# Pool stage: the expert sums of the last two token tiles by two VectorE operations each, one of them ahead of the first pooling

## The reference

```python
y = lax.map(run_block, (xin, blk_e)).reshape(P, D)               # experts, each token's two rows
out = jnp.zeros((N, D), x.dtype).at[tok_pad].add(y * w_pad[:, None])   # sum of the two, by their gates
...
h = layer_norm(DEEPNORM_ALPHA * h + ffn, ln_g[i, 1], ln_b[i, 1])
...
u = (x @ w_in).reshape(B, S, N_POOL_GROUPS, POOL_GROUP_DIM)      # pool_mixer, x is that h
for g, w in enumerate(POOL_WINDOWS):                             # windows of 2, 4, 8, 16 tokens
    ...
    mean = (cs - lag) / jnp.minimum(count, float(w))[None, :, None]
    feats.append(mean - ug)
y = jnp.einsum('bsgc,gcd->bsgd', p, w_grp).reshape(B, S, D_MODEL) * ls
```

## Time and profile before

| | |
|---|---|
| median of 3 runs | 3607.46 us (3605.31 to 3608.38) |
| profiled execution, its own time | 3608.5 us |
| its span in the profile | 3606.6 us |
| PE, DVE, ACT busy, share of the span | 95%, 67%, 52% |
| stage with the change | about 1293 to 1509 us of the span |

### The profile page before, as it was taken

One profiled execution on the slowest core, in us unless ns is written; L12 is line 12 of the kernel. 1 busy time (PEld: TensorE's weight loads), 2 busy tenths in 40 slices (PEclk: granted clock), 3 DMA queues, 4 the chain that ended last, 5 costly groups with the idle time before them and its releaser, 6 DMA issues. The chain is left out here.

```text
span 3606.6 us, 53860 instructions
## 1 busy us (share of the span) xinstructions
PE 3428.8 (95%) x18205; PEld 2678.3 (74%) x18205; DVE 2410.1 (67%) x3983; ACT 1873.4 (52%) x3187; POOL 430.8 (12%) x499
## 2 busy tenths in 40 slices
PE   8998889899999989998999999899999999999988
PEld 7885658688888845686888887477887768787866
DVE  3226877699998957647999888664077655416776
ACT  3215662288888821114888887232167633215764
POOL 0000002011111130000111111410000310000032
PEclk9999999899999999998999999999999999999999
DMA  6643225299999976544999998643242333424142
GB/s 242 227 149 95 71 79 187 93 384 388 378 373 377 360 268 245 199 176 164 381 384 378 378 371 328 235 150 137 72 124 75 128 131 131 168 72 127 43 159 70
DMA packets 416290, 766.17 MB, mean 212 GB/s; under 512 B 107609, under 2 KB 166641, under 8 KB 414072
## 3 DMA queue, kind: packets, MB, share of 16 engines
q1 hardware_dynamic: 393080, 711.93, 55.3%
q0 software_dynamic: 22752, 50.93, 3.8%
q10 hardware_dynamic: 288, 1.05, 0.1%
HBM read 643.00 MB, written 152.72 MB: 221 GB/s over the span
## 5 line engine op out<-in xcount | busy, mean ns | idle before, releaser
L253 DVE TENSOR_TENSOR experts_gate_lo<-weights_gate,experts_gate_hi 128x1024 fp32r<-128x1024 f32 x256 | 301.5, 1221 | 71.5 <-ACT experts_gate_hi L249 71.1
L253 DVE TENSOR_TENSOR experts_down_lo<-weights_down,experts_down_hi 128x1024 fp32r<-128x1024 f32 x256 | 296.2, 1219 | 34.2 <-ACT experts_down_hi L249 34.2
L249 ACT CAST experts_gate_hi<-weights_gate 128x1024 fp32r<-128x1024 f32 x256 | 255.7, 1056 | 110.3 <-DMA weights_gate<-in_moe_w_gate_dram 75.2
L253 DVE TENSOR_TENSOR experts_up_lo<-weights_up,experts_up_hi 128x1024 fp32r<-128x1024 f32 x256 | 295.9, 1218 | 0.3
L318 PE MATMUL project_acc<-project_wh,project_hh 128*128 128x512 f32 (+2 forms) x768 | 286.7, 373 | 0.0
L320 PE MATMUL project_acc<-project_wh,project_hl 128*128 128x512 f32 (+2 forms) x768 | 282.9, 368 | 0.0
L319 PE MATMUL project_acc<-project_wl,project_hh 128*128 128x512 f32 (+2 forms) x768 | 282.9, 368 | 0.0
L249 ACT CAST experts_up_hi<-weights_up 128x1024 fp32r<-128x1024 f32 x256 | 256.0, 1057 | 11.1 <-DMA weights_up<-in_moe_w_up_dram 9.3
L249 ACT CAST experts_down_hi<-weights_down 128x1024 fp32r<-128x1024 f32 x256 | 253.8, 1053 | 6.9 <-DMA weights_down<-in_moe_w_down_dram 6.8
L2855 ACT COPY project_row<-project_acc 128x512 f32<-128x512 f32 (+2 forms) x96 | 51.8, 540 | 365.8 <-PE project_acc L320 365.8
L318 PE MATMUL experts_gp<-experts_gate_hi,experts_xh 128*128 128x512 f32 x512 | 202.4, 395 | 10.9 <-DVE experts_xl L253 10.9
(11 more groups left out here) (560 smaller groups left out, 8190.9 us busy)
## 6 DMA issues: line engine op xcount, KB each, us to landing
weights_gate<-in_moe_w_gate_dram SPq DMA_DIRECT2D x256, 512.0 KB, 11.9
weights_up<-in_moe_w_up_dram SPq DMA_DIRECT2D x256, 512.0 KB, 13.2
weights_down<-in_moe_w_down_dram SPq DMA_DIRECT2D x256, 512.0 KB, 11.4
scratch_y<-qkv_zero SPq DMA_DIRECT2D x48, 512.0 KB, 4.4
pool_shared<-in_ada_w_dram SPq DMA_DIRECT2D x16, 1536.0 KB, 7.9
scratch_proj<-project_row SPq DMA_DIRECT2D x64, 256.0 KB, 2.0
head_store<-in_attn_w_qkv_dram SPq DMA_DIRECT2D x48, 256.0 KB, 3.5
scratch_qkv<-qkv_row SPq DMA_DIRECT2D x48, 256.0 KB, 2.0
```

Of the source, the lines that this page charges most:

```text
L249: return act.copy(hi, src)
L253: return dve.tensor_tensor(lo, src, hi.bitcast(F32), ALU.subtract)
```

## The change

For tiles 6 and 7 the diagonal matrices and the PE sums are gone. ACT scales the loaded h by ALPHA in place (`scale_h`), ahead of copy_u 0 and copy_u 1 in its list. DVE then forms r from SBUF by two operations of 1024 columns, the second on the result of the first. DVE's list is in another order: norm 5 directly behind norm 4, then tile 6's add, window 0, norm 6, tile 7's add, window 1, norm 7, outputs 0, window 2. The modulation's first load waits for the adds and no longer for the PE sums, which stands in the list behind the last store as before.

```diff
+    def scale_h(self, act, i):
+        u = i % self.HB
+        act.wait_ge(self.h_in[u], 16 * (i // self.HB) + 16)
+        act.activation(self.hin[:, u, :], self.hin[:, u, :], ACT.Copy, scale=ALPHA).then_inc(self.h_scaled, 1)
...
-        for c in range(2):
+        if i >= self.DIRECT:
+            v = i % self.YB
+            dve.wait_ge(self.h_scaled, i - self.DIRECT + 1)
+            dve.wait_ge(self.y_in[v], 32 * (i // self.YB) + 32)
+            ch(dve.scalar_tensor_tensor(r, self.yin[v][:, 0, :], self.gates[:, 0, i:i + 1], self.hin[:, u, :], ALU.mult, ALU.add))
+            ch.wait()
+            dve.scalar_tensor_tensor(r, self.yin[v][:, 1, :], self.gates[:, 1, i:i + 1], r, ALU.mult, ALU.add).then_inc(self.r_taken, 2)
+        for c in range(2 if i < self.DIRECT else 0):
...
-                            sp.wait_ge(cb.rp_ready, 2 * TILES)
+                            sp.wait_ge(cb.r_taken, 2 * TILES)
...
                     channels(n)
-                    cb.sums(nc, pe, n + 2 + HT)
                     transposes(n + HT)
...
-                for i in range(TILES):
+                for i in range(cb.DIRECT):
                     cb.diagonals(act, i)
...
                 for n in range(STEPS):
+                    if n < TILES - cb.DIRECT:
+                        cb.scale_h(act, n + cb.DIRECT)
                     copy_u(n)
...
+                norm(HT + 1)
+                cb.add(dve, cch, HT + 2)
                 dve.wait_ge(small_in, 16 * (2 * NG + 1))
-                for n in range(2):
-                    window(n)
-                    cb.add(dve, cch, n + HT + 2)
-                    norm(n + HT + 1)
+                window(0)
+                norm(HT + 2)
+                cb.add(dve, cch, HT + 3)
+                window(1)
+                norm(HT + 3)
...
-                        if n == CG:
-                            norm(TILES - 1)
```

More of the change, by code:

```diff
@@ L2022, with __init__ @@
     YB = 3
-    def __init__(self, ph, K, ahead, y, gates, dest_i, out, yin, r, hn, banks, diagonals, narrow=TILES):
-        self.NARROW = narrow
+    def __init__(self, ph, K, ahead, y, gates, dest_i, out, yin, r, hn, banks, diagonals, narrow=TILES, direct=TILES):
+        self.NARROW, self.DIRECT = narrow, direct
         self.K, self.y, self.gates, self.dest_i, self.out = K, y, gates, dest_i, out
@@ L2032, in __init__ @@
         self.rstd, self.half = ph.sb("cb_rstd", [P, 2, 1]), ph.sb("cb_half", [P, 1])
-        (self.idx_ready, self.diag_ready, self.rp_ready, self.r_taken, self.ms_ready, self.rstd_ready,
+        (self.h_scaled, self.idx_ready, self.diag_ready, self.rp_ready, self.r_taken, self.ms_ready, self.rstd_ready,
          self.h_ready, self.own) = (ph.sem(f"cb_{n}") for n in (
-            "idx_ready", "diag_ready", "rp_ready", "r_taken", "ms_ready", "rstd_ready", "h_ready", "own"))
+            "h_scaled", "idx_ready", "diag_ready", "rp_ready", "r_taken", "ms_ready", "rstd_ready", "h_ready", "own"))
         self.y_in = [ph.sem(f"cb_y_in{u}") for u in range(self.YB)]
@@ L2271, in phase_combine_pool @@
         cb = Combine(ph, K, ahead, y, gates, dest_i, out, [yin[:, n] for n in range(Combine.YB)],
-                     [r[:, n] for n in range(2)], [hn[:, n] for n in range(2)], [rp[:, n, :] for n in range(4)], ph.sb("diag", [P, TILES * 2 * P])[:, :], HT)
+                     [r[:, n] for n in range(2)], [hn[:, n] for n in range(2)], [rp[:, n, :] for n in range(4)], ph.sb("diag", [P, TILES * 2 * P])[:, :], HT, TILES - 2)
         yp = rp[:, 0:2, :]
```

## The result

The changed kernel takes 3612.32 us in the median of 22 runs, before 3608.39 in 22 runs: a ratio of 1.0013, 95% interval 1.0007 to 1.0019, so 2.5 to 6.9 us slower. The profiled execution after took 3614.8 us with a span of 3612.6, against 3608.5 and 3606.6.

What follows compares the result with a forecast made beforehand. PE, busy 170.84 of 170.90 us in the stage, was taken as the bound. Outputs 0 3.8 us late plus 2.7 us of low clock gave + 6.5: 3615.0 against the profiled execution, 3614.0 against the median; 8-in-10 range 3609.8 to 3617.

Steps and rivals of the forecast that it cites:

- PE no longer does 6.9 us: On PE, the sums of tiles 6 and 7, 3.44 us each, go; PE reaches outputs 0 6.6 us earlier.
- DVE's chain: DVE's operations up to window 1 end at 1370.4, so outputs 0 start 3.8 us late after PE idles 10.4 us.
- item 2: Before tile 6's add: h lands at 1349.7, 8.7 us after issue, ACT scales in 1.07 us, DVE starts at 1350.8.
- Transposes 5 held up by ACT: On PE before channels 2: ACT, delayed by scaling, frees the bank's second half at about 1352.6; transposes end at about 1353.1.
- The clock: Behind PE's idle time: 5.60 us at 1.2 GHz cost 2.7 us on outputs 0, transposes 6 and the head of channels 3.
- Sum: Whole kernel: 3.8 us late start plus 2.7 us clock, + 6.5 us, time 3614.0; chance 0.65.
- Behind outputs 0 nothing else: From outputs 0 to the next stage PE works without gaps and the shift is carried whole; no further term.
- The full gain: Rival at the wait before outputs 0: window 1 written by about 1360.0, 6.6 us gained, 3600.9; chance 0.05.
- an add that starts right behind norm 5: Tile 6's add on DVE at 1343.7: window 0 held by counts to 1348.36, chain ends at 1363.5, -3.1 with clock kept.

Runs made afterwards that it cites:

- e3: The change with tile 6's h loaded early and DVE forming both windows before norm 6 and tile 7's add: channels 0 to channels 3 26.75 us, ratio 0.9974 to before.
- e12: e5 with norm 5 moved directly behind norm 4: channels 0 to channels 3 on PE 30.18 us, ratio 0.9993 to before.
- e1: The change with 10 throwaway matmuls on PE ahead of the wait for window 1: channels 0 to channels 3 35.66 us, ratio 1.0010 to before.
- e10: The changed kernel profiled a second time, nothing altered: channels 0 to channels 3 on PE 39.19 us, one execution of 3613.19 us.
- e9: The kernel before profiled a second time, nothing altered: channels 0 to channels 3 on PE 33.62 us, one execution of 3603.66 us.
- e5: The change with only tile 7's sum on DVE, tile 6's on PE, norm 6 ahead of tile 7's add: channels 0 to channels 3 33.11 us, ratio 1.0003.
- e8: The change with windows 0 and 1 ahead of tile 6's add, no load moved: channels 0 to channels 3 28.23 us, ratio 0.9992 to before.
- e11: e3 timed and profiled a second time: channels 0 to channels 3 on PE 26.76 us, ratio 0.9974 to before.
- e4: The kernel before with only DVE's list in the change's order, sums still on PE: channels 0 to channels 3 33.62 us, ratio 0.9997 to before.
- e2: The change with tile 6's load of h issued some 10 us sooner: channels 0 to channels 3 on PE 32.56 us, ratio 0.9993 to before.

## Why the prediction was right, by its steps

- *PE no longer does 6.9 us.* Right: 6.87 in e3, 3.44 for one tile in e12.
- *DVE's chain.* Right in its order and nearly in size. Outputs 0 were to start 33.1 us behind channels 0 (1370.4 - 1337.3) and started at 32.45. Most of the difference is item 2: ACT began to scale at 11.80 and not at 12.4; the chain behind it took 19.3 us for 19.6. That item 2 came so close is partly luck, as two misses in it offset each other: the load landed 7.3 us after its issue for the 8.7 taken from before, but was issued 4.5 us behind channels 0 for 3.7. ACT's scaling, 1.07 in the sum, took 1.29 from its start to DVE's. The late start is 3.15 us for the 3.8 forecast.
- *Transposes 5 held up by ACT.* Wrong, without consequence: they follow channels 1 at once, at 1351.48, since ACT had emptied the bank by then (its last copy of tile 4 ended at 1351.17). The recorded text also disagrees with itself here: its own sum delays the end of these transposes by 0.2 us (1353.1 for 1352.0 + 0.87), while item 2 speaks of 1.1. PE stood before outputs 0 at 22.4 us behind channels 0 instead of 22.7; it stood still for 9.86 us where 10.4 were forecast.
- *The clock.* Right as a mechanism (e1 takes it away), 2.13 us for 2.7, and 2.46 in the second profile (e10): the low level ended inside outputs 0, earlier than in the stretch that I took as model.
- *Sum.* + 5.28 in the yardstick, against + 6.5; the median moved by 3.9 (2.5 to 6.9). The rest of the stage was + 1.6 longer in the first pair of profiles, which e9 shows to be within what it does by itself. The time itself came 1.7 us below the forecast of 3614.0, the shift 2.6 us below; that the time is the closer one is luck, since the 3 runs that I started from, with a median of 3607.46, lay 0.9 below the 22.
- *Behind outputs 0 nothing else.* Right in the profile: no idle time of PE behind L2398 up to the next stage. Other profiles have waits of 0.3 to 0.7 us for later windows there: one each in e5, e8, e10, e11 and e12, two each in e1 and in e4, which has its sums on PE. Before has none in either profile.
- *The rivals.* The full gain needed DVE 10 us sooner. I had named shorter operations as the only way; e3 and e8 show another, which the list had in it: putting tile 7's add and norm 6 behind window 1. My figure for an add that starts right behind norm 5 was good for the wait and wrong for the clock: 3.1 us sooner than before with the clock kept, while e2 started outputs 0 2.6 us sooner and then lost 1.6 us to the clock. That I bounded this rival with the order given is right for the change and would mislead as advice.

The cause of the 5.28 us is shown by e1, e2, e3 and e8: the wait for the load of tile 6's h, which holds its add and all of DVE's list behind it, then norm 6 and tile 7's add in front of window 1, plus the clock.

## What to carry to other kernels

As long as the other engines' lists stay as they are, work taken off the busiest engine is worth no more than the smallest room at its waits, here 4.9 us before the first outputs and 1.0 before transposes 5: list every wait of the relieved engine with that room before moving work, the small ones too. In the list of the engine that takes the work over, put first what the relieved one waits for first; with norm 6 and tile 7's add in front of window 1 and the late load ahead of both, the kernel was 3.9 us slower than before; with them behind it and the early load it was 9.1 us faster, of which the yardstick accounts for 6.9. An operation that needs a late load belongs behind those that don't.

## What the runs showed of the hardware

- With 4.07 us of idle time (e2) the clock fell as it did with 9.86 (the change): outputs 0 took 5.03 and 5.58 us instead of 3.45, and 5.91 with 9.82 us of idle time in e10. The longer idle time cost only 0.55 to 0.88 us more through the clock.
- Two shorter waits cost no clock: it was 1.00 in and behind the 2.71 us of e5 and the 1.26 us of e8, and the channels behind them took their usual 7.03 us. In the gap of the change it was 1.00 from 1359 to 1363 and 0.52 from 1363 to 1367; in e2's gap the mean was 0.95.
- The clock falls inside or behind the modulation's totals too, 48 records of matmuls with one column, though PE's records touch throughout: before's first total, from 1440.60, ran at 1.00 up to 1443, at 0.81 to 1446.5, and the channels behind it at 0.51 up to 1452.1. In e9 the second total ran at 1.00 whole, and the outputs behind it at a mean of 0.67; in the first profile of before the level was 0.50 from 1493 on, inside the total. So their cost moves from run to run: the stretch to the last transposition was 10.5 us in one profile of before and 13.8 in the other.
- DVE's first direct operation of tile 6 and the dependent second were 1.39 us apart, start to start (1349.88 to 1351.27), 0.07 more than a norm's pair (1.32); for float32 in SBUF, two inputs of 1024 columns, the operation itself lasts 1.28 to 1.29 us as the norm's do.
